# Differential attention with memory heads first and heads 4 to 7 projected by tokens, and a memory preparation in two parts

## The chip, the cores and the metric

The kernel runs on one core of one Trainium2 chip. The metric is the device time of one execution in microseconds (us), the median of several runs. The engines are named as in the profile: PE is TensorE (PEld its weight loads), DVE is VectorE, ACT is ScalarE, POOL is GpSimd and SP is SyncE, which here only issues transfers. A change of 0.2% is 2.8 us.

## The reference, cut to what matters

The program is a stack of transformer blocks on 256 tokens of width 1024, with feed-forward layers (d_ff 2816) and a different mixer in each block. The change touches the second mixer, differential attention with memory heads, and in one place the mixer after it, whose block prepares a second memory.

```
def diff_layer(h, w_in, lam_p, norm_g, w_out, mem_k, mem_v, slopes, layer_idx):
    proj = h @ w_in
    q = proj[..., :DIFF_QK].reshape(B, S, H, 2, Dh).transpose(0, 2, 3, 1, 4)
    k = proj[..., DIFF_QK:2 * DIFF_QK].reshape(B, S, H, 2, Dh).transpose(0, 2, 3, 1, 4)
    v = proj[..., 2 * DIFF_QK:2 * DIFF_QK + DIFF_V].reshape(B, S, H, 2 * Dh).transpose(0, 2, 1, 3)
    xq = proj[..., 2 * DIFF_QK + DIFF_V:]
    ...
    o = diff_attention(q, k, v, lam, slopes)     # per head: softmax(q0 k0) - lam * softmax(q1 k1), times v
    o = rmsnorm(o, norm_g, eps=SUBLN_EPS) * (1.0 - lam_init)
    o = o.transpose(0, 2, 1, 3).reshape(B, S, H * 2 * Dh)
    xo = memory_attention(xq, mem_k, mem_v)      # 4 heads of 128 against 256 memory rows
    return jnp.concatenate([o, xo], axis=-1) @ w_out
```

There are H = 8 heads, each with two components of Dh = 64, and h has 1024 features. All is float32.

## The kernel before

**Weights come in chunks.** Every weight matrix is cut into chunks of 128 x 2048 floats (1 MB), 234 in all. SP loads a chunk into one of three `raw` buffers; ACT rounds it to `w_hi` (L1493), and DVE writes the rest to `w_lo` (L1743), each in rings of three. PE multiplies three times for each tile: high by high, high by low, low by high.

**A chunk is used in one of two forms.** By columns (`columns_chunk`, L1134 to L1136) the weights are stationary and 256 tokens move, so that features come out on the partitions; one chunk holds 256 output columns and takes 48 products of 128x256 into one `prod` bank. DVE scales the bank by `rb` (the norm of each token, spread over the partitions by a small product and a copy, `spread`) and writes `q`, `k` or `xq`. By tokens (`tokens_chunk`, L1140 to L1144) the activations are stationary and 512 weight columns move, so that tokens come out on the partitions; two chunks (the halves of the 1024 features) give 512 output columns in two banks, one for each 128 tokens, with 24 products of 128x512 a chunk. ACT scales the banks by the token's norm (L1558) and writes `v`. The output projection (`down_chunk`) is by tokens too.

**Attention is cut into ticks.** `Plan.ticks` makes a pipeline over heads: a tick holds scores (S, L1338), the weights on DVE (F), the turning of the weights on PE (T, L1358) and its copy on ACT (L1678), the product with v (V, L1379 to L1397), and the low part of a finished memory tile on DVE (L, L1855). A differential head scores both components in one tick, in `acc` banks 0 and 1, each with 64 of the 128 rows of the array; the next tick has no scores. PE runs a tick in the middle of a chunk (`mid`) and one behind it (`end(slot)`). In the stage of the output projection (`pl.draining`), where the `acc` banks are taken, a tick scores one component at a time in `prod` bank 0. `HeadNorms` puts the norm of each head (ACT squares, POOL root, DVE scale) and, by pairs, the turning of the outputs (L1472) around the ticks.

**The order of the differential layer** is written out in `make_plan`: query and key of heads 0 and 1 by columns, the values of heads 0 to 3 by tokens (two chunks), query and key of heads 2 and 3, the values of heads 4 to 7, query and key of the last two pairs, two chunks of `xq`, and six chunks of output projection. Heads 0 to 7 come first in the ticks and the four memory heads last; these are scored between the chunks of the output projection. Before the layer stands `prep`, which turns x to features in four banks while DVE and ACT write `acts_h` (L1520) and `acts_l` (L1770).

**Moving by blocks.** In the feed-forward layers a middle tile is turned without PE: DVE transposes squares of 32 x 32 (L1904), and 16 transfers of 32 partitions, 8 issued by SP and 8 by POOL (`move_blocks`, L1004), put the squares on their partitions.

**In the mixer after it** `mem_prep` readies four tiles of the second memory ahead of the gate chunks (`rg`): ACT writes the high parts (L1668) and DVE the low parts (L1994); behind it DVE scales x (L2001), writes the `w_lo` of a chunk, and then the low part of an attention tile (L1855) for which PE's next V waits.

All engines take their work in the order of one list of items, and wait on semaphores.

Of the kernel before, what the change touches and what calls it, by code (L numbers as in the profile page):

```python
# [26 lines left out]
P = 128  # L27
D = 1024
# [93 lines left out]
class Plan:  # L122


    def __init__(self):
# [23 lines left out]
        self.early_half = False  # L149
        self.quartered = None  # L150
# [65 lines left out]
    def prep(self, gain, resid, last_down=None, double=False, wait=False):  # L216
        it = self.add("prep", gain=gain, resid=resid, first=self.acts, acts_free=self.acts_users,
                      x_new=self.x_new, y=self.y, y_chunk=self.y_chunk, x_turned=self.x_turned, n=self.stat,
                      double=double, wait=wait)
# [13 lines left out]
    def mem_prep(self, gain, kts, tiles, source):  # L233
        self.add("mem_prep", gain=gain, kts=kts, tiles=tiles, source=source, first=self.mem,
                 users=self.c if source == "mem2" else 0)
        self.mem += len(kts)

# [84 lines left out]
    def project_tokens(self, source, col, dest, at, of="x", mid=None, between=None):  # L322
        for k_half in range(2):
            self.chunk("rows_half", (*source, "half", (k_half, col)), mid, e=self.e, k_half=k_half, dest=dest, at=at,
                       of=of, acts=self.acts if of == "x" else self.mem, free=self.bank_free(2))
# [13 lines left out]


# [74 lines left out]
    def ready(self, units):  # L415
        for unit in units:
            unit["need"], unit["rope"] = self.read, self.rope_n
# [31 lines left out]
def unit_of(head, **k):  # L449
    return dict(dict(head=head, comps=1, tiles=1, v_width=P, out_tiles=1, out_row=0, tile=head, need=None,  # L450
                     need_v=None, is_out=False, closes=True, free=lambda: True, half=head % 2), **k)


def mem_units(heads, dims, q, layer=0):
    tiles = dims // P
    return [unit_of(h, shape=FULL, table=None, scale=1.0, q=(q, h * tiles),
# [5 lines left out]
class HeadNorms:  # L462
# [10 lines left out]
    def early(self):  # L473
        if self.scales >= 2 * (self.turns + 1) and not self.hold_turn:
            self.pl.head_turn(self.turns, self.which)
            self.turns += 1

    def late(self):
        if self.splits < self.turns:
            self.pl.head_lo(self.splits, self.which)  # L480
# [29 lines left out]
def make_plan():  # L510
# [77 lines left out]
    for _ in down:  # L588
# [10 lines left out]
    memory = mem_units(4, P, "xq", 1)  # L599
    heads = [unit_of(h, comps=2, shape=CAUSAL, table="alibi", scale=2.0 ** -(h + 1), q=("q", h), k=("k", h),  # L600
                     rows=None, v=("v", h * P), out="norm") for h in range(HEADS)]
    norms = HeadNorms(pl, heads, "diff")
    ticks = pl.ticks([[unit] for unit in heads + memory])
# [14 lines left out]
    query(0, None)  # L618
    pl.spread("x")
    key(0, None)  # L620
    pl.ready(heads[0:2])
    value(0)
    query(1)
    end(slot)
    key(1)
    end(slot)
    pl.ready(heads[2:4])
    value(2)
    for pair in (2, 3):
# [5 lines left out]
    for n in range(2):  # L635
        pl.project(w, 3 * D + n * COLS, "xq", 2 * n, mid=slot, factors=(P ** -0.5,) * 2)
        end(slot)
    pl.ready(memory)
    pl.ready_v(memory)
    pl.draining = True  # L640
    norms.hold_turn = True

    def memory_turned(n):
        if n == 2:
            norms.hold_turn = False

    downs(slot, "diff_w_out", 0, pairs_of(0, 1, 2, 4, 5, 3), memory_turned)
# [1598 lines left out]
```

## Time and profile before

| | us |
|---|---|
| median of 3 runs | 1418.22 (1418.0 to 1418.61) |
| the profiled execution, its time | 1418.27 |
| its span, first to last instruction | 1416.5 |
| PE busy | 1403.6 |
| differential layer on PE (683.65 to 826.61) | 142.96 |

The matmul durations of the profile overlap: a product of 128x512 lasts 0.39 us, but the next starts 0.23 us after it. What a chunk costs is therefore read from the starts of its products, not from their durations. The granted clock of PE is 0.999 of full speed over the span.

### The profile page before, as it was taken

What the parts mean: (1) busy time and instruction counts of PE and PEld (TensorE: products, weight loads), DVE (VectorE), ACT (ScalarE), POOL (GpSimd) and SP (SyncE); (2) the same over time, 40 slices, a digit from 0 to 9 for tenths busy, and PEclk for the clock granted to TensorE, in tenths of its full rate; (3) what the DMA queues carried; (4) which work ended last, traced back from release to release, by engine and by line L of the source; (5) the groups of instructions that cost most, each with busy time, mean ns of one, the idle gap of its engine ahead of it and who ended that gap; (6) DMA issues with size and microseconds to landing.
All of it is one profiled execution on the core that took longest, in us unless ns stands there. A gap on an engine that the chain in (4) does not pass through costs nothing.

```text
span 1416.5 us, 18653 instructions
## 1 busy us (share of the span) xinstructions
PE 1403.6 (99%) x7200; PEld 1190.3 (84%) x7200; DVE 857.3 (61%) x1035; ACT 704.9 (50%) x981; POOL 259.8 (18%) x504
## 2 busy tenths in 40 slices
PE   9999999999999999999999999999999999999998
PEld 7888889988888888888889888888887989888886
DVE  5656565756555565555656565555796655565554
ACT  6554454445444454444555555444555554644443
POOL 1022210002222222222012113222201100132222
PEclk9999999999999999999999999999999999999999
DMA  9765654455655656665544446665553553366562
GB/s 349 290 213 201 219 186 156 166 185 192 221 201 198 218 196 215 207 220 198 180 149 150 139 168 258 216 222 200 186 177 136 188 179 134 125 228 225 197 220 74
DMA packets 71655, 275.55 MB, mean 195 GB/s; under 512 B 17392, under 2 KB 37232, under 8 KB 40848
## 3 DMA queue, kind: packets, MB, share of 16 engines
q1 hardware_dynamic: 57168, 259.57, 51.6%
q0 software_dynamic: 14400, 14.81, 3.4%
q8 instruction: 57, 0.93, 0.3%
q14 instruction: 30, 0.25, 0.0%
HBM read 259.88 MB, written 1.05 MB: 184 GB/s over the span
## 4 chain that ended last, share of the span: by engine, by line
PE 95%; ACT 2%; DVE 1%; issue 1%; DMA 0%; POOL 0%; SPq 0%; DVEq 0%; POOLq 0%; ACTq 0%
PE prod L1140 16%; PE prod L1141 16%; PE prod L1144 15%; PE acc L1144 10%; PE acc L1140 10%; PE acc L1141 10%; PE prod L1134 5%; PE prod L1136 5%; PE prod L1135 5%; PE acc L1338 1%; PE acc L1159 1%; ACT w_hi L1493 1%; PE acc L1358 1%; DVE w_lo L1743 0%; PE o_bank L1394 0%
## 5 line engine op out<-in xcount | busy, mean ns | idle before, releaser
L1743 DVE TENSOR_TENSOR w_lo<-raw,w_hi 128x2048 fp32r<-128x2048 f32 x233 | 533.6, 2291 | 383.4 <-ACT w_hi L1493 380.8
L1493 ACT CAST w_hi<-raw 128x2048 fp32r<-128x2048 f32 x233 | 444.2, 1907 | 431.6 <-PE prod L1144 182.1
L1140 PE MATMUL prod<-w_hi,acts_h 128*128 128x512 f32 x944 | 370.2, 392 | 2.5 <-DVE w_lo L1752 1.8
L1144 PE MATMUL prod<-w_hi,acts_l 128*128 128x512 f32 x944 | 367.7, 389 | 0.0
L1141 PE MATMUL prod<-w_lo,acts_h 128*128 128x512 f32 x944 | 367.4, 389 | 0.0
L1004 POOL DMA_DIRECT2D four<-four x408 | 200.1, 498 | 602.4 <-DVE four L1904 585.3
L1140 PE MATMUL acc<-w_hi,mix_h 128*128 128x512 f32 x600 | 236.0, 393 | 0.0
L1144 PE MATMUL acc<-w_hi,mix_l 128*128 128x512 f32 x600 | 233.7, 390 | 0.0
L1141 PE MATMUL acc<-w_lo,mix_h 128*128 128x512 f32 x600 | 233.5, 389 | 0.0
L1140 PEld LDWEIGHTS prod<-w_hi,acts_h 128*128 128x128 f32 x944 | 177.2, 188 | 43.0 <-issue 6.9
L1144 PEld LDWEIGHTS prod<-w_hi,acts_l 128*128 128x128 f32 x944 | 177.2, 188 | 37.5 <-DVE acts_l L1814 0.3
L1141 PEld LDWEIGHTS prod<-w_lo,acts_h 128*128 128x128 f32 x944 | 177.3, 188 | 35.6
L1144 PEld LDWEIGHTS acc<-w_hi,mix_l 128*128 128x128 f32 x600 | 112.6, 188 | 23.7
L1140 PEld LDWEIGHTS acc<-w_hi,mix_h 128*128 128x128 f32 x600 | 112.7, 188 | 23.0
L1141 PEld LDWEIGHTS acc<-w_lo,mix_h 128*128 128x128 f32 x600 | 112.7, 188 | 22.6
L1134 PE MATMUL prod<-acts_h,w_hi 128*128 128x256 f32 x424 | 124.0, 293 | 1.1 <-ACT work L1558 0.7
L1136 PE MATMUL prod<-acts_h,w_lo 128*128 128x256 f32 x424 | 119.9, 283 | 0.0
L1135 PE MATMUL prod<-acts_l,w_hi 128*128 128x256 f32 x424 | 119.8, 283 | 0.0
L1573 ACT ACTIVATE four<-prod,stats 128x256 f32<-128x256 f32 x108 | 51.1, 474 | 115.4 <-PE prod L1144 103.3
L1134 PEld LDWEIGHTS prod<-acts_h,w_hi 128*128 128x128 f32 x424 | 81.1, 191 | 3.6 <-issue 2.4
L1074 POOL TENSOR_SCALAR stats<-stats 128x1 f32<-128x1 f32 x28 | 14.1, 505 | 373.9 <-ACT sq L1506 372.8
L1135 PEld LDWEIGHTS prod<-acts_l,w_hi 128*128 128x128 f32 x424 | 81.2, 191 | 0.4 <-issue 0.2
(277 smaller groups left out, 1261.7 us busy)
## 6 DMA issues: line engine op xcount, KB each, us to landing
raw<-in_weights_dram SPq DMA_DIRECT2D x234, 1024.0 KB, 5.0
four<-four SPq DMA_DIRECT2D x408, 16.0 KB, 2.1
four<-four POOLq DMA_DIRECT2D x408, 16.0 KB, 1.9
raw<-in_weights_dram SPq DMA_DIRECT2D x16, 256.0 KB, 6.9
work<-in_mem_dram POOLq DMA_DIRECT2D x2, 1024.0 KB, 13.5
grow<-in_gain_rows_dram POOLq DMA_DIRECT2D x4, 512.0 KB, 3.7
tabs<-in_tabs_dram POOLq DMA_DIRECT2D x1, 1632.0 KB, 9.9
work<-in_x_t_dram SPq DMA_DIRECT2D x4, 256.0 KB, 5.7
```

Of the source, the lines that this page charges most:

```text
L1004: engine.dma_start(mid_moved_to[32 * b:32 * b + 32, a * P:(a + 1) * P], mid_blocks[32 * a:32 * a + 32, b * P:(b + 1) * P]).then_inc(done, 16)
L1134: pe.matmul(out, wh, moving_hi, start=first, stop=False, skip_group_check=True)
L1135: pe.matmul(out, wh, moving_lo, start=False, stop=False, skip_group_check=True)
L1136: return pe.matmul(out, wl, moving_hi, start=False, stop=last, skip_group_check=True)
L1140: pe.matmul(out, still_hi, wh, start=first, stop=False, skip_group_check=True)
L1141: pe.matmul(out, still_hi, wl, start=False, stop=False, skip_group_check=True)
L1144: return pe.matmul(out, still_lo, wh, start=False, stop=last, skip_group_check=True)
L1159: mm = pe.transpose(bank[:, i * S + t * P:i * S + (t + 1) * P], x[:, t, kt * P:(kt + 1) * P], ident)
L1338: mm = pe.matmul(bank[:, at:at + width], dests[q][r0:r1, qt + n, t * P:(t + 1) * P], dests[k][r0:r1, kt + n, 0:width], start=(n == 0), sto ...
L1493: act.copy(w_hi[:, c % RING], raw[:, c % RAW]).then_inc(hi_done, 1)
L1573: act.activation(gate_s[:, t], up_bank(it, t)[:, 0:S], ACT.Silu, scale=rstd["x"][:, t:t + 1]).then_inc(silu_done, 1)
L1743: dve.tensor_tensor(w_lo[:, c % RING], raw[:, c % RAW], w_hi[:, c % RING].bitcast(F32), ALU.subtract).then_inc(lo_done, 1)
```

## The change

1. **Three projections go by tokens, and are turned to features afterwards.** `project_turned` replaces six chunks by columns (two of `xq`, two of q and two of k, for heads 4 to 7) with six by tokens. ACT writes the two banks, scaled, to a buffer `cut` (in `mem_k`) in groups of 32 columns; DVE transposes all squares of 128x1024 in one instruction into a second buffer (in `obuf`); 16 transfers of 32x256 (8 from SP, 8 from POOL) move them to `xq`, `q` or `k`. For keys (`keys=True`) the transpose writes runs of 32 neighbouring elements; for queries (`xq`, q) it writes every eighth element, and PE loads such a query tile with a step of eight floats (`tokens_of`), while keys are read in runs of 32 (`keys_of`).
2. **Factors.** Queries need a factor for each head: POOL makes products of the norm and the factor (`scales`, one for `xq`, four for q).
3. **Order.** `xq`, q and k of heads 4 to 7, their values, then q, k of heads 0 and 1, values of heads 0 to 3, q and k of heads 2 and 3, then the output projection in the order of pairs 4, 5, 2, 3, 0, 1. In the ticks the memory heads come first, then heads 4 to 7, then 0 to 3. `spread` moves behind the values.
4. **Memory preparation in two parts.** The low parts on DVE become an item of their own (`mem_low`), put behind the first gate chunk.
5. Waits on the transfers are added for the scores and for whatever overwrites what they read.

```diff
@@ class Plan
+    def project_turned(self, source, col, dest, at, buffers, keys, of="x", mid=None, between=None, scales=None):
+        for k_half in range(2):
+            self.chunk("rows_half", (*source, "half", (k_half, col)), mid, e=self.e, k_half=k_half, dest=dest, at=at,
+                       of=of, acts=self.acts if of == "x" else self.mem, free=self.bank_free(2), turned=self.turned,
+                       buffers=buffers, scales=scales, keys=keys)
...
+        self.turn_behind[self.c + RAW] = self.items[-1]
+        self.turned += 1
+        for t in range(2):
+            self.bank_reader.append(("cut_done", 2 * self.turned - 1 + t))
@@ make_plan, the differential layer
-    ticks = pl.ticks([[unit] for unit in heads + memory])
+    heads_in_order = heads[4:8] + heads[0:4]
+    ticks = pl.ticks([[unit] for unit in memory + heads_in_order])
...
+    pl.project_turned(w, 3 * D, "xq", 0, "diff", False, scales=pl.scales([P ** -0.5]))
+    pl.ready(memory)
+    pl.ready_v(memory)
+    pl.project_turned(w, 512, "q", 4, "diff", False,
+                      scales=pl.scales([2.0 ** (h + 1) * 64 ** -0.5 for h in range(4, 8)]))
+    end(slot)
+    pl.project_turned(w, D + 512, "k", 4, "diff", True, mid=slot, between=lambda: end(slot))
+    end(slot)
+    pl.project_tokens(w, 2 * D + 512, "v", 512, mid=slot, between=lambda: end(slot))
...
-    downs(slot, "diff_w_out", 0, pairs_of(0, 1, 2, 4, 5, 3), memory_turned)
+    downs(slot, "diff_w_out", 0, pairs_of(4, 5, 2, 3, 0, 1))
@@ make_plan, the gate chunks
-    pl.mem_prep("g_mem", [4, 5, 6, 7], [8, 9, 10, 11], "mem2")
+    prepared = pl.mem_prep("g_mem", [4, 5, 6, 7], [8, 9, 10, 11], "mem2", low=False)
     pl.add("scale_x", stat=pl.stat)
-    pl.project_tokens(w, 2560, "rg", 0, mid=slot, between=lambda: end(slot))
+
+    def gate_half():
+        end(slot)
+        pl.mem_low(prepared)
+
+    pl.project_tokens(w, 2560, "rg", 0, mid=slot, between=gate_half)
@@ build
+        def tokens_of(name, blocks, rows, tile, t):
+            if not blocks:
+                return dests[name][rows, tile, t * P:(t + 1) * P]
+            four_tiles = dests[name][:, tile // 4 * 4:tile // 4 * 4 + 4].rearrange("p a b -> p (a b)")
+            return four_tiles.rearrange("p (i t k) -> p k t i", t=2, k=4)[rows, tile % 4, t]
+
+        def move_features(engine, it, token_blocks, done):
+            to = dests[it["dest"]][:, it["at"]:it["at"] + 4].rearrange("p a b -> p (a b)")
+            engine.wait_ge(features_turned, it["turned"] + 1)
+            for a in token_blocks:
+                for b in range(4):
+                    engine.dma_start(to[32 * b:32 * b + 32, a * S:(a + 1) * S],
+                                     cut_buffer(it, 1)[32 * a:32 * a + 32, b * S:(b + 1) * S]
+                                     ).then_inc(done, 16)
@@ scores on PE
+                    if unit["moved"]:
+                        pe.wait_ge(early_features_moved, 128 * unit["moved"])
+                        pe.wait_ge(late_features_moved, 128 * unit["moved"])
@@ vector
+                        dve.wait_ge(cut_done, 2 * it["turned"] + 2)
...
+                        dve.transpose(blocks, cut).then_inc(features_turned, 1)
```

**DVE, the start of the differential layer, before.** From the last low activation tile on: `work` is q and k of heads 0 and 1, and L1867 is the mask and maximum of the first scores.

```order
L1770 SCALAR_TENSOR_TENSOR acts_l<-acc3,vecs,acts_h 128x256
L1743 TENSOR_TENSOR w_lo<-raw,w_hi 128x2048 [waits hi_done]
L1922 SCALAR_TENSOR_TENSOR work<-prod0,rb 128x256 [waits chunk_used,rb_done]
L1922 SCALAR_TENSOR_TENSOR work<-prod0,rb 128x256
L1743 TENSOR_TENSOR w_lo<-raw,w_hi 128x2048 [waits hi_done]
L1916 TENSOR_TENSOR work<-prod1,rb 128x512 [waits chunk_used,rb_done]
L1743 TENSOR_TENSOR w_lo<-raw,w_hi 128x2048 [waits hi_done]
L1867 ISA masked,small<-tabs,acc0 128x128 [waits score_done]
```

And after, from the same place: L2029 are the transposes of `xq` and of q, L1976 the maximum of the first memory head.

```order
L1883 SCALAR_TENSOR_TENSOR acts_l<-acc3,vecs,acts_h 128x256
L1856 TENSOR_TENSOR w_lo<-raw,w_hi 128x2048 [waits hi_done] x2
L2029 STREAM_TRANSPOSE obuf<-mem_k 128x4x8x32 [waits cut_done]
L1856 TENSOR_TENSOR w_lo<-raw,w_hi 128x2048 [waits hi_done] x2
L2029 STREAM_TRANSPOSE obuf<-mem_k 128x4x8x32 [waits late_features_moved,early_features_moved,cut_done]
L1976 TENSOR_REDUCE small<-acc0 128x2 [waits score_done]
L1856 TENSOR_TENSOR w_lo<-raw,w_hi 128x2048 [waits hi_done]
L1942 RECIPROCAL small<-small 128x2 [waits exp_done]
```

Two reads of `prod` banks for each pair of heads have become one transpose for each four tiles, and the first maximum stands directly behind a transpose that waits for ACT's cut.

**PE, the first chunk of the output projection, after.** `work` is q and k of head 2; `acc` is the projection; in the rows of before this stage scored only memory heads (`prod0<-mem_k,obuf`).

```order
L1225 MATMUL acc1<-w_hi,mix_l 128x512
L1422 MATMUL prod0<-work 128x128 [waits prod_read,max_done,late_features_moved,early_features_moved]
L1422 MATMUL prod0<-work 128x256
L1464 MATMUL prod1<-work,four 128x128 [waits prod_read,hn_scaled,turned_read,values_read]
L1465 MATMUL prod1<-work,four 128x128
L1466 MATMUL prod1<-work,four 128x128
L1221 MATMUL acc2<-w_hi,mix_h 128x512 [waits hn_scaled,turned_read]
```

The two components of heads 2 and 3 have moved into this stage, where each is scored alone, one at a stop: four stops with one component in place of two with both.

**DVE, the gate chunks, before.** L1994 is the low part of the memory, L2001 the scaling of x, L1855 the low part for which PE's V waits.

```order
L1855 TENSOR_TENSOR mix_l<-o_bank,mix_h 128x256 [waits o_hi]
L1994 SCALAR_TENSOR_TENSOR mix_l<-obuf,vecs,mix_h 128x256 [waits mem_hi] x4
L2001 TENSOR_SCALAR x_res<-x_res,stats 128x1024 [waits rstd_done,xf_done]
L2001 TENSOR_SCALAR x_res<-x_res,stats 128x1024
L1743 TENSOR_TENSOR w_lo<-raw,w_hi 128x2048 [waits hi_done,dve_step]
L1855 TENSOR_TENSOR mix_l<-acc3,mix_h 128x256 [waits o_hi]
```

And after:

```order
L1968 TENSOR_TENSOR mix_l<-o_bank,mix_h 128x256 [waits o_hi]
L2125 TENSOR_SCALAR x_res<-x_res,stats 128x1024 [waits rstd_done,xf_done]
L2125 TENSOR_SCALAR x_res<-x_res,stats 128x1024
L1856 TENSOR_TENSOR w_lo<-raw,w_hi 128x2048 [waits hi_done,dve_step]
L1968 TENSOR_TENSOR mix_l<-acc3,mix_h 128x256 [waits o_hi]
L1937 TENSOR_TENSOR four<-acc0,tabs 128x384 [waits turned,score_done]
L1937 TENSOR_TENSOR sq<-acc1,tabs 128x384 [waits o_done,score_done]
L2118 SCALAR_TENSOR_TENSOR mix_l<-obuf,vecs,mix_h 128x256 [waits mem_hi] x4
```

The four memory tiles have gone behind the low part that PE waits for.

## Rows read from the trace of the kernel before

**Rows 1.** The page, section 1: engine, busy us, share of span, instructions.

```profile
PE 1403.6 (99%) x7200; PEld 1190.3 (84%) x7200; DVE 857.3 (61%) x1035; ACT 704.9 (50%) x981; POOL 259.8 (18%) x504
```

**Rows 2.** Timeline of PE at four chunk starts: start, length, instruction.

```profile
860.61 0.39 PE L1140 MATMUL acc<-w_hi,mix_h 128*128 128x512 f32 x1
...
866.05 0.39 PE L1140 MATMUL prod<-w_hi,acts_h 128*128 128x512 f32 x1
...
1119.20 0.28 PE L1134 MATMUL prod<-mix_h,w_hi 128*128 128x256 f32 x1
...
1142.24 0.40 PE L1140 MATMUL prod<-w_hi,mix_h 128*128 128x512 f32 x1
```

**Rows 3.** What PE waited for: total us, times, longest.

```profile
PE acc L1379 <- DVE mix_l L1855: 0.9, 1, 0.9
PE prod L1134 <- ACT work L1558: 0.7, 1, 0.7
...
PE prod L1134 <- DVE acts_l L1770: 0.4, 2, 0.2
```

**Rows 4.** Timelines of PE and PEld at one head's scores and one memory head's.

```profile
699.93 0.93 PE L1338 MATMUL acc<-work 64*128 64x128 f32 x8
700.78 0.50 PE L1140 MATMUL prod<-w_hi,acts_h 128*128 128x512 f32 x1
...
700.25 0.38 PE L1338 MATMUL acc<-work 64*128 64x256 f32 x2
...
700.47 0.38 PE L1338 MATMUL acc<-work 64*128 64x256 f32 x2
...
700.14 0.20 PEld L1338 LDWEIGHTS acc<-work 64*128 64x128 f32 x2
...
700.26 0.20 PEld L1338 LDWEIGHTS acc<-work 64*128 64x128 f32 x2
...
785.44 1.02 PE L1338 MATMUL prod<-mem_k,obuf 128*128 128x256 f32 x4
786.30 0.27 PE L1358 MATMUL aux<-tabs,four 128*128 128x128 f32 x1
```

**Rows 5.** Groups by line and form: busy us, mean ns, idle before; then two DMA issues.

```profile
L1743 DVE TENSOR_TENSOR w_lo<-raw,w_hi 128x2048 fp32r<-128x2048 f32 x233 | 533.6, 2291 | 383.4 <-ACT w_hi L1493 380.8 <-POOL stats L1077 2.2
L1493 ACT CAST w_hi<-raw 128x2048 fp32r<-128x2048 f32 x233 | 444.2, 1907 | 431.6 <-PE prod L1144 182.1 <-PE acc L1144 166.8 <-PE prod L1136 76.2
L1004 POOL DMA_DIRECT2D four<-four x408 | 200.1, 498 | 602.4 <-DVE four L1904 585.3 <-issue 16.9
L1904 DVE STREAM_TRANSPOSE four<-four 128x512 f32<-128x512 f32 x51 | 36.3, 712 | 1.8
L1558 ACT ACTIVATE work<-prod,stats 128x512 f32<-128x512 f32 x8 | 5.2, 678 | 4.5 <-PE prod L1144 4.5
L1686 ACT ACT_TABLE_LOAD x4 | 5.1, 1283 | 0.1
L1863 DVE TENSOR_REDUCE small<-acc 128x2 f32<-128x512 f32 x7 | 4.8, 687 | 2.0 <-PE acc L1338 2.0
L1686 ACT ACTIVATE four<-acc,small 128x256 f32<-128x256 f32 x10 | 4.7, 474 | 3.9 <-DVE small L1863 3.7
L1678 ACT COPY four<-acc 128x512 f32<-128x512 f32 x6 | 3.5, 586 | 11.9 <-PE acc L1358 11.9
...
four<-four SPq DMA_DIRECT2D x408, 16.0 KB, 2.1
four<-four POOLq DMA_DIRECT2D x408, 16.0 KB, 1.9
```

**Rows 6.** Timelines of ACT, DVE and PE around the gate chunks, 1080 to 1089 us.

```profile
1080.34 1.90 ACT L1493 CAST w_hi<-raw 128x2048 fp32r<-128x2048 f32 x1
...
1082.95 1.68 DVE L1994 SCALAR_TENSOR_TENSOR mix_l<-obuf,vecs,mix_h 128x256 fp32r<-128x256 f32 x4 [5.64 <-ACT mix_h L1668]
...
1088.20 0.42 DVE L1855 TENSOR_TENSOR mix_l<-acc,mix_h 128x256 fp32r<-128x256 f32 x1
```

More of the change, by code:

```diff
@@ L231, in prep, with mem_prep, mem_low @@
             self.statistic("x", "x")
[L233 to L235 removed]
+    def mem_prep(self, gain, kts, tiles, source, low=True):
+        it = self.add("mem_prep", gain=gain, kts=kts, tiles=tiles, source=source, first=self.mem,
+                      users=self.c if source == "mem2" else 0)
         self.mem += len(kts)
+        if low:
+            self.mem_low(it)
+        return it
+    def mem_low(self, of):
+        self.add("mem_low", of=of)
     def post_norm(self, gain):
@@ L474, in early @@
         if self.scales >= 2 * (self.turns + 1) and not self.hold_turn:
-            self.pl.head_turn(self.turns, self.which)
+            self.pl.head_turn(self.units[2 * self.turns]["head"] // 2, self.which)
             self.turns += 1
@@ L598, in make_plan @@
     w = ("diff_w_in", 0)
-    memory = mem_units(4, P, "xq", 1)
+    memory = mem_units(4, P, "xq", 1, q_blocks=True)
     heads = [unit_of(h, comps=2, shape=CAUSAL, table="alibi", scale=2.0 ** -(h + 1), q=("q", h), k=("k", h),
-                     rows=None, v=("v", h * P), out="norm") for h in range(HEADS)]
-    norms = HeadNorms(pl, heads, "diff")
-    ticks = pl.ticks([[unit] for unit in heads + memory])
+                     rows=None, v=("v", h * P), out="norm", q_blocks=h >= 4, k_blocks=h >= 4) for h in range(HEADS)]
+    heads_in_order = heads[4:8] + heads[0:4]
+    norms = HeadNorms(pl, heads_in_order, "diff")
+    ticks = pl.ticks([[unit] for unit in memory + heads_in_order])
     slot = slots(ticks, norms)
@@ L616, in value @@
         pl.ready_v(heads[2 * pair:2 * pair + 4])
-    query(0, None)
-    pl.spread("x")
[L620 to L629, printed above, removed]
+    pl.project_turned(w, 3 * D, "xq", 0, "diff", False, scales=pl.scales([P ** -0.5]))
[7 more added lines that the diff above has]
+    pl.project_tokens(w, 2 * D + 512, "v", 512, mid=slot, between=lambda: end(slot))
+    pl.ready(heads[4:8])
+    pl.ready_v(heads[4:8])
+    end(slot)
+    pl.spread("x")
+    for pair in range(2):
         query(pair)
@@ L634, in make_plan @@
         pl.ready(heads[2 * pair:2 * pair + 2])
[L635 to L639, printed above, removed]
-    pl.draining = True
[L641 to L645, printed above, removed]
-    downs(slot, "diff_w_out", 0, pairs_of(0, 1, 2, 4, 5, 3), memory_turned)
+        if pair == 0:
+            value(0)
+    pl.draining = True
+    downs(slot, "diff_w_out", 0, pairs_of(4, 5, 2, 3, 0, 1))
     pl.draining = False
@@ L1100, in _ @@
                     move_blocks(pool, (2, 3), late_blocks_moved)
+                elif kind == "rows_half" and it["k_half"] and it.get("turned") is not None:
+                    move_features(pool, it, (2, 3), late_features_moved)
+                elif kind == "scales":
+                    pool.wait_ge(rstd_done, it["stat"])
+                    for n, factor in enumerate(it["factors"]):
+                        ins = pool.tensor_scalar(scales[:, 2 * (it["at"] + n):2 * (it["at"] + n) + 2], rstd["x"], factor,
+                                                 None, ALU.mult)
+                    ins.then_inc(scales_done, len(it["factors"]))
                 elif kind == "load_mem2":
```

97 lines of the change are left out of this document (85 added, 12 removed).

## The prediction, written before the changed kernel was run

> **What bounds the kernel now.** I read the shares of the engines first. PE is busy in 99% of the span [rows 1], so the time is PE's work in order plus its few waits, and any other engine costs only where PE waits for it. But a busy PE is not yet a price: its products overlap. So I read second, on the timeline, how far apart the starts of chunks lie. From 860.61 to 866.05 PE does one chunk by tokens, 24 products of 128x512, in 5.44 us. From 1119.20 to 1142.24 it does four chunks by columns, 192 products of 128x256, in 23.04 us: 5.76 us each [rows 2]. The durations in the groups would have said something else; the starts decide. Third, the list of PE's waits [rows 3]. Three of them lie where the change works: 0.4 us for the low activations and 0.7 us for ACT's write of v, both in the differential layer, and 0.9 us for a low attention tile in the gate chunks. They are single waits, so all that the change can give lies in the price of chunks and in these three.
>
> **Part 1, six chunks by tokens.** 6 x (5.44 - 5.76) = -1.9 us [rows 2]. All of it is on the path. This is small because the form by columns moves as many elements in all; only the cost of a start is saved.
>
> **Part 2, the wait for low activations.** By columns PE needs all eight activation tiles within one chunk; by tokens the first chunk needs four, and the second four are due 6.3 us after the layer's start, where I find them written after 5.7 us. The 0.4 us [rows 3] go: -0.4. The turning of the second half of x now stands 2.7 us into the chunk and finds its data there.
>
> **Part 3, the wait for v.** PE waited 0.7 us at a `prod` bank because ACT had exponentials of two heads, and earlier a table load of 1.28 us [rows 5], ahead of L1558. In the new order no tick stands in the last chunk of the first values, so ACT is free there; behind the second values the pattern is that of before, which had no wait. With a little of the switch, -0.8 us.
>
> **Part 4, the gate chunks.** DVE sat idle 5.64 us until ACT had written the memory's high parts, then did four low parts in 1.68 us, then the rest, and came to PE's tile at 1088.20 [rows 6]. The high weights were there since 1080.34 + 1.90 = 1082.24. Without the memory, DVE scales x in the idle time, starts `w_lo` at 1082.3, needs 2.29 us [rows 5] and is at PE's tile at about 1084.6, over 3 us before PE asks. The 0.9 us [rows 3] go. The four low parts come after the tick; the next `w_lo` is needed two chunks (10.9 us) later, so 1.7 us are covered, and nothing else reads them before the memory projection. If that cover were gone, they would cost 1.7 us. -0.9 us.
>
> **Part 5, scores of heads 2 and 3 between the chunks of the output projection.** The scores of a head with both components take 700.78 - 699.93 = 0.85 us [rows 4]. They run in pairs: two products start together at 700.25 and two at 700.47, one of each component, since each takes half of the array's rows. A component alone has no partner, but as many steps: it costs from 0.65 us (the steps 0.11, 0.11, 0.22, 0.22 of the pairs' starts) to 0.85. Four alone instead of two pairs: 4 x 0.65 - 1.7 = +0.9 to 4 x 0.85 - 1.7 = +1.7. I take the middle, +1.3, and +0.1 for one more interruption of the stream.
>
> **Part 6, new waits in the phase of the memory heads.** Times count from the layer's start on PE. This is where ACT and DVE get the most new work, and I walk it by rows 5. Projections of `xq` end at 11.8. ACT cuts (0.68 us a bank) by 12.6; the transpose has twice the elements of L1904, 0.71 us, so I estimate 1.25 us (0.53 us more for 512 more elements at the pace of 128 lanes that the row allows): 13.9. POOL issues 8 transfers of 0.5 us, to 18, and landing adds 1.9: 20. SP's eight wait behind a chunk and are as early. The first memory scores are due at 22.7, so this wait is hidden by q's two chunks with 2.7 us to spare. Behind POOL's transfers stand four factor products; they end at 20 to 22, when ACT wants to cut q at 20.0; that cut is due at 23.5. Queued behind SP's wait is the next chunk's load, which lands 1 to 4 us early even so.
>
> Then it becomes tight. ACT cuts q to 24.0, writes a `w_hi` of 1.9 to 25.9 and loads its table to 27.2; DVE waits for the cut, transposes to 25.3 and gives the first maximum (0.69) at 26.0; exponentials (two of 0.47 and their sums, 1.35) end at 28.6; the weights are ready at 29.5, PE turns them at 30.7. Each further memory head takes ACT 1.35 + 0.59 us and a small cast, and DVE its maximum, two multiplications and a low part, an estimate of 2 us, every 4 us of PE, beside 1.9 and 2.3 us for every chunk of 5.4. ACT reaches the cut of k only behind the fourth exponentials, at 39.2, and finishes its first bank at 39.9; PE wants that bank at 39.8, +0.2. The second V wants the first output's low part, which on DVE stands behind k's transpose: ready at 43.2, wanted at 42.7, +0.55. Together +0.75. After that PE does two chunks with hardly a tick and all catch up; the transfers of k land by 48, and head 4 is scored at 53. From below: both waits vanish if ACT is 0.6 us faster, 0. From above: each of the four ticks late by a `w_hi` share, as in the one wait of 0.7 us that ACT's queue makes now [rows 3], 4 x 0.7 = +2.8.
>
> **Part 7, queries read with a step of eight floats.** No row shows such a load. The nearest are the packed ones: a pair of loads starts 0.12 us after the one before [rows 4], and they feed products 0.22 us apart. From below 0, since they are hidden; if a load took twice as long, 0.24 us, it would still be hidden but for the two first products of a head and the first load of a memory head: about +0.25 for each of heads 4 to 7 and +0.1 for each memory head, +1.4. The packed row is the nearest, but nothing says that the step is free; I take +0.2.
> The Trainium skill (SBUF — State Buffer, Door 1: The DMA port swizzle) has a rule against this: SBUF has lines of 16 bytes, and every access that goes to a new line pays, so that float32 may step four elements at most for free. It gives no figure. By it part 7 is not near 0 but at the +1.4 of a doubling or above; it is the rival below.
>
> **The sum.** -1.9 - 0.4 - 0.8 - 0.9 + 1.3 + 0.1 + 0.75 + 0.2 = -1.65 us. The profiled execution took 1418.27 us (span 1416.5 and 1.8 around it) and is within 0.05 of the median 1418.22, so the forecast is 1416.6 us. A measurement of this kernel tells about 0.2%, 2.8 us, from no change: below 1415.4 is faster, above 1421.1 slower. The forecast is the same within that.
>
> **Rivals.**
> Faster: the new waits are nil and a component alone costs 0.65 us. -1.9 - 0.4 - 0.8 - 0.9 + 0.9 + 0.1 = -3.0, 1415.2 us; with the over-heads of switching between the two forms saved, 1414.5. For it: PE's queue shows only three waits in the whole stage before, and memory heads between projection chunks already run at one tick for each half chunk without one. Against: there ACT had no cut and no table load.
> Queues: ACT and DVE fall behind in the memory phase by the upper end, +2.8 instead of +0.75, and part 5 costs 1.7: 1416.6 + 2.05 + 0.4 = 1419.1 us. For it: the margins of part 6 are 0.1 to 2 us on a walk of 20 steps. A transpose that writes every eighth element slower than L1904 would do it, 1.25 us each time.
> Slower, the strided loads: one mechanism, at L1422 for the queries of heads 4 to 7 and of memory. The loads come to bind once one takes longer than the 0.22 us of its product, that is from a doubling of 0.12. At three times (0.33 to 0.36) a head costs 4 x 0.33 = 1.32 instead of 0.65, a memory head 1.32 instead of 0.86: 4 x 0.67 + 4 x 0.46 = +4.5, 1420.9 us; at four times +8, 1424.5. For it: nothing in the trace excludes it; against: the stage's loads are hidden twofold now.
> That the chunks do not get cheaper: then the transfers' and cuts' waits eat 1.9 us and it ends at 1418.5. The two prices come from long clean stretches, so this is unlikely, and I fold it into the queues.
>
> **How the numbers follow.** Forecast, 1415.5 to 1418: 0.47. Queues, 1418 to 1420.5: 0.20. Faster, 1413.5 to 1415.4: 0.21. Strided loads at three times or more: 0.12. Faster by over 0.2%: 0.21. Slower by over 0.2%: most of the strided case and a tail of the queues, 0.14. Within 0.2%: 0.65. The range for 8 in 10 runs from 1413.9 to 1420.8: it leaves out the far half of the strided case and the ends of the others.
>
> **What would show it.** Right: chunks of `xq`, q and k by tokens 5.44 us apart in starts; no PE wait for L1883 in the layer's first two chunks, none at the gate chunks; each of the four lone components of heads 2 and 3 at 0.65 to 0.85 us; waits of under 1 us in all between 20 and 50 us of the layer; scores of heads 4 to 7 at 0.85 to 1.1 us. Wrong: memory scores far over 0.86 us or heads 4 to 7 far over 0.85 (the step), PE waiting for DMA at the first memory scores (the transfers), for ACT's cuts at k's or the values' chunks or for a `mix_l` (the queues), or a wait in the last two projection chunks, where the norm of heads 2 and 3 now has less than a chunk and a half.

## The result and the profile after

The changed kernel takes 1423.54 us, the median of 5 runs (1423.2 to 1424.76), against 1418.19 us for the kernel before in the same session: a ratio of 1.0036, 95% interval 1.0025 to 1.0047. That is 5.3 us (0.4%) slower, outside the predicted range, whose upper end was 1420.8. The profiled execution took 1423.2 us, span 1421.4.

The page's section 1 of the changed kernel, and what its PE waited for (total us, times, longest):

```profile
PE 1407.9 (99%) x7056; PEld 1187.6 (84%) x7056; DVE 857.1 (60%) x1030; ACT 709.9 (50%) x993; POOL 265.3 (19%) x533
```

```profile
PE prod L1221 <- DVE four L2013: 3.8, 1, 3.8
...
PE prod L1215 <- DVE acts_l L1883: 0.2, 1, 0.2
```

The shares are within one point of those of [rows 1]. Of the three waits of [rows 3] the one for v and the one for the low tile at the gate chunks are gone. Of the one for low activations the half in the differential layer (0.2 us, at 687.93) is gone too; the other half stood in a later layer (at 1013.21) that the change leaves alone, and it is the 0.2 us that is left (at 1019.01). One wait is new and larger than all three together, and it does not lie in the layer that was changed: it is in the feed-forward layer behind it. The differential layer itself takes 143.8 us on PE (starts 683.55 to 827.37), against 143.0 before; the first stretch of the next layer takes 35.55 us (830.92 to 866.47) for chunks that take 30.48 before. So +0.9 us in the layer that was rewritten and +5.1 us behind it; less the 0.9 us that is gone at the gate chunks this comes to 5.1 us, and the spans of the two profiled executions differ by 4.9.

**Where the 3.8 us are made.** In that layer DVE transposes a block at 840.42, SP and POOL move it with eight transfers each, and ACT casts it. ACT's queue has this cast ahead of its read of the next projection (L1683); DVE's read of the same bank (L2013) follows, and only then is the bank free for PE's next projection. So PE does not wait for the moved tiles themselves, but for a bank whose readers stand behind them. The timelines of POOL, SP, ACT, DVE and PE of the changed kernel there:

```profile
843.96 4.03 POOL L1075 DMA_DIRECT2D four<-four  x8 [11.55 <-issue]
...
846.15 3.42 SPq L1106 DMA_DIRECT2D raw<-in_weights_dram  x2
...
852.11 0.71 ACT L1598 CAST mix_h<-four 128x256 fp32r<-128x256 f32 x2 [5.22 <-DMA four<-four]
852.73 0.83 ACT L1683 ACTIVATE four<-prod,stats 128x256 f32<-128x256 f32 x2
...
853.53 0.87 DVE L2013 SCALAR_TENSOR_TENSOR four<-prod,stats,four 128x256 f32<-128x256 f32 x2
...
854.15 0.77 PE L1221 MATMUL prod<-w_hi,acts_h 128*128 128x512 f32 x1 [3.83 <-DVE four L2013]
...
854.72 0.63 PE L1222 MATMUL prod<-w_lo,acts_h 128*128 128x512 f32 x1
```

and of POOL, SP and ACT of the kernel before, whose transpose ran at 839.62:

```profile
840.62 4.01 POOL L1004 DMA_DIRECT2D four<-four  x8 [8.99 <-DVE four L1904]
...
845.35 3.43 SPq L1035 DMA_DIRECT2D raw<-in_weights_dram  x2
...
846.56 0.71 ACT L1513 CAST mix_h<-four 128x256 fp32r<-128x256 f32 x2 [0.47 <-DMA four<-four]
```

Before, POOL starts 0.3 us behind the end of the transpose, released by it. After, it starts 2.8 us behind the end (841.13), and the view has only "issue" as what it waited for: the data were there and POOL did nothing. Its last three transfers (846.51 to 847.5) are issued behind SP's next weight load of 1 MB (846.15). They land only after that load has landed (851.5), 4.5 to 5.0 us after their issue; before, all of POOL's transfers were issued ahead of the load, and the longest of the move took 2.2. So 2.5 us on POOL become 4.7 at ACT's cast, counted from each kernel's transpose.

PE then pays twice. Its granted clock, by the view of windows (stretch, length, PE busy, clock, DMA share, GB/s):

```profile
852.00:854.00 2.00, 0.00 (x0) 0.90 0.69 291
854.00:856.00 2.00, 1.85 (x5) 0.50 0.04 8
856.00:858.00 2.00, 2.00 (x8) 0.75 0.20 44
858.00:860.00 2.00, 2.00 (x11) 1.00 0.24 59
```

After 3.8 us without work PE runs at 1.2 GHz, half of its clock, until 857: products start 0.43 us apart instead of 0.23 (854.72 to 855.14). That is the further 1.2 us of the 5.07.

**Why POOL was idle.** I counted the transfers that POOL issues, from 0, in both traces. In each, POOL stands still for about 3 us ahead of numbers 133 and 261. Before, number 261 is a load of the memory, that nobody waits for (timeline of POOL before, where the number before it is the last of the row above):

```profile
862.84 3.91 POOL L1004 DMA_DIRECT2D four<-four  x8 [7.34 <-DVE four L1904]
870.25 0.56 POOL L1103 DMA_DIRECT2D work<-in_mem_dram  x1 [3.49 <-issue]
```

The change lets POOL issue 24 transfers for xq, q and k. With them, number 261 is the first transfer of the first block move behind the layer. That is a correlation of two traces; the experiments put it to the test.

### The profile page after: what moved, and what is told of

It reads as the page before. It is cut to its first block, busy times and chain, and to the rows that moved or that the text cites. A ratio compares the mean times of both kernels' runs of the same rounds, so it can differ in the third digit from the quotient of the medians.

```text
span 1421.4 us, 18464 instructions
## 1 busy us (share of the span) xinstructions
PE 1407.9 (99%) x7056; PEld 1187.6 (84%) x7056; DVE 857.1 (60%) x1030; ACT 709.9 (50%) x993; POOL 265.3 (19%) x533
## 4 chain that ended last, share of the span: by engine, by line
PE 97%; DVE 1%; DMA 1%; issue 0%; ACT 0%; POOL 0%; SPq 0%; DVEq 0%; POOLq 0%; ACTq 0%
PE prod L1221 17%; PE prod L1225 17%; PE prod L1222 17%; PE acc L1221 10%; PE acc L1225 10%; PE acc L1222 10%; PE prod L1215 4%; PE prod L1217 4%; PE prod L1216 4%; PE acc L1422 2%; PE acc L1240 1%; PE acc L1443 1%; PE o_bank L1479 0%; PE o_bank L1482 0%; PE prod L1422 0%
## 5 line engine op out<-in xcount | busy, mean ns | idle before, releaser
L1221 PE MATMUL prod<-w_hi,acts_h 128*128 128x512 f32 x992 | 390.6, 394 | 4.8 <-DVE four L2013 3.8
L1225 PE MATMUL prod<-w_hi,acts_l 128*128 128x512 f32 x992 | 387.0, 390 | 0.0
L1222 PE MATMUL prod<-w_lo,acts_h 128*128 128x512 f32 x992 | 386.7, 390 | 0.0
L1221 PEld LDWEIGHTS prod<-w_hi,acts_h 128*128 128x128 f32 x992 | 186.7, 188 | 47.6 <-issue 9.8
L1222 PEld LDWEIGHTS prod<-w_lo,acts_h 128*128 128x128 f32 x992 | 186.7, 188 | 37.5
L1683 ACT ACTIVATE four<-prod,stats 128x256 f32<-128x256 f32 x108 | 51.0, 475 | 117.3 <-PE prod L1225 105.4
L1215 PE MATMUL prod<-acts_h,w_hi 128*128 128x256 f32 x328 | 96.0, 293 | 0.2 <-DVE acts_l L1883 0.2
L1217 PE MATMUL prod<-acts_h,w_lo 128*128 128x256 f32 x328 | 92.7, 283 | 0.0
L1216 PE MATMUL prod<-acts_l,w_hi 128*128 128x256 f32 x328 | 92.7, 283 | 0.0
L2013 DVE SCALAR_TENSOR_TENSOR four<-prod,stats,four 128x256 f32<-128x256 f32 x108 | 51.7, 481 | 34.6 <-ACT four L1683 32.6
L1215 PEld LDWEIGHTS prod<-acts_h,w_hi 128*128 128x128 f32 x328 | 62.8, 191 | 1.4 <-issue 0.7
```

Of the source, the lines that this page charges most:

```text
L1215: pe.matmul(out, wh, moving_hi, start=first, stop=False, skip_group_check=True)
L1216: pe.matmul(out, wh, moving_lo, start=False, stop=False, skip_group_check=True)
L1217: return pe.matmul(out, wl, moving_hi, start=False, stop=last, skip_group_check=True)
L1221: pe.matmul(out, still_hi, wh, start=first, stop=False, skip_group_check=True)
L1222: pe.matmul(out, still_hi, wl, start=False, stop=False, skip_group_check=True)
L1225: return pe.matmul(out, still_lo, wh, start=False, stop=last, skip_group_check=True)
```

## Experiments on the new wait

**24 transfers in the kernel before, and 24 memsets as a control.** Everything else is as before.

```diff
     pl.prep("norm_g11", 0.5, pl.last_down)
+    pl.add("pad", n=24)
...
+                elif kind == "pad":
+                    for n in range(it["n"]):
+                        pool.dma_start(spare[0:32, 4 * n:4 * n + 4], tabs[0:32, 16:20]).then_inc(padded_done, 16)
```

The control has `pool.memset(spare[:, n:n + 1], 0.0)` there.

> The kernel before, with 24 small transfers (32 rows of 16 bytes, into a spare buffer that nobody reads) issued by POOL ahead of the differential layer, and nothing else of the change. In both traces POOL issues nothing for about 3 us ahead of its transfers number 133 and 261 (counted from 0). In the changed kernel number 261 is the first transfer of the first block move of the feed-forward layer behind the differential layer, and PE waits 3.83 us for that move; in the kernel before number 261 falls elsewhere. Theory A (every 128th transfer that POOL issues is held up for some 3 us, and the 24 feature transfers that POOL issues for q, k and xq moved this point onto the move): these 24 transfers do the same to the kernel before, its first move there is 3 us late, PE waits 3 to 5 us on its products, and the time is 1421.2 to 1423.3 us. Theory B (the wait comes from the new order of the differential layer, its clock, its weight loads or its reads): 1418.2 us, within 0.5.

> The kernel before, with 24 POOL memsets of one column each in the place where the run with 24 transfers has its transfers. Theory A (the hold-up goes by POOL's transfers): their number is that of the kernel before, POOL's hold-up stays where it was, 1418.2 us within 0.5. Theory C (it goes by the length of POOL's instruction stream, which is fetched in pieces, so that any 24 more instructions move it): POOL's hold-up moves too, and the time is 1419 to 1423 us.

Measured: 1425.14 us with the transfers (ratio 1.0045, 1.0032 to 1.0058), 1418.88 with the memsets (1.0001, 0.9993 to 1.0010). PE's waits and POOL's timeline with the transfers:

```profile
PE prod L1147 <- DVE four L1907: 4.0, 1, 4.0
...
843.74 4.01 POOL L1007 DMA_DIRECT2D four<-four  x8 [11.52 <-issue]
```

and what POOL waited for with the memsets:

```profile
POOL work L1108 <- issue: 3.0, 1, 3.0
```

Nothing of the changed layer is in this kernel, and it shows the same wait at the same move. With the memsets the hold-up stays at the load of the memory. So it goes by transfers, not by the length of POOL's stream: theory A stands, B and C fall. The time came out above theory A's upper end by 1.8 us. The half clock behind the wait gives most of it, by the windows of this kernel:

```profile
854.00:856.00 2.00, 1.93 (x5) 0.50 0.03 8
856.00:858.00 2.00, 2.00 (x6) 0.50 0.24 56
858.00:860.00 2.00, 2.00 (x7) 0.67 0.25 59
```

The half clock lasts until past 859 here (products start 0.43 us apart up to 859.33, in the changed kernel up to 856.85), and from 856 to 860 PE starts 10 products where it starts 15 in the changed kernel: 5 x 0.23 = 1.2 us. (The counts of the windows are higher, since a product that runs across the edge counts in both.) The wait is only 0.1 us longer. Nor is it a matter of the kernel alone: two of its five executions took 1423.93 us, the other three 1425.14 to 1425.57. What such a stall costs is thus not fixed by its length, and what decides it stays open.

**One transfer more in the changed kernel.** The same edit with n=1 (and rows of 64 bytes).

> The changed kernel, with one small transfer more (32 rows of 64 bytes, into a spare buffer) issued by POOL ahead of the differential layer. Theory A (by the number of the transfer): the first transfer of the feed-forward layer's first move is number 262 now, number 261 is the last feature transfer of k, some 5 us ahead of its reader, so PE's wait of 3.83 us on L1221 goes and the time is 1418.0 to 1419.5 us. Theory B (the new order of the layer) and theory C (the length of the stream, changed by one instruction): 1423.5 us, within 0.5.

Measured: 1418.26 us (0.9998, 0.9989 to 1.0006), 5.3 less than the changed kernel. POOL's timeline at the end of k's feature move and at the block move:

```profile
725.33 3.45 POOL L1041 DMA_DIRECT2D work<-obuf  x7 [10.71 <-DVE obuf L2036]
731.20 0.50 POOL L1041 DMA_DIRECT2D work<-obuf  x1 [2.42 <-issue]
...
841.31 4.02 POOL L1078 DMA_DIRECT2D four<-four  x8 [8.98 <-DVE four L2024]
```

The hold-up has gone to the eighth transfer of k, which is number 261 now, and nobody waits there: it lands at 734.27, and the first scores that read it start at 737.42. A kernel with one useless instruction more is 5.3 us faster; PE's stretch from 830.81 on takes 30.47 us, as before the change. This is the clearest proof that the whole step of 5.1 us belongs to that one number.

**What is counted: transfers or rows.** 24 transfers of one row (`spare[0:1, ...]`) instead of 32.

> The run with 24 small POOL transfers in the kernel before, each of them of 1 row instead of 32. Theory A1 (the hold-up comes at every 128th transfer, whatever its size): as with 32 rows, the first transfer of the move behind the differential layer is number 261, PE waits 3 to 5 us for the move, 1423 to 1425 us. Theory A2 (it comes at every 4096th row, that is descriptor, of POOL's transfers, and 128 moves of 32 rows make up that number): 24 rows shift it by less than one transfer, the hold-up stays where the kernel before has it, 1418.5 us within 0.6.

Measured: 1423.91 us (1.0039, 1.0025 to 1.0053). POOL's timeline:

```profile
843.46 4.03 POOL L1007 DMA_DIRECT2D four<-four  x8 [11.52 <-issue]
```

24 rows or 768, the same transfer is late: theory A1. It is the number of transfers.

**What it costs at other places.** 8 and 16 transfers instead of 24.

> The kernel before with 8 small POOL transfers (32 rows) ahead of the differential layer. POOL's transfer number 261 is then the first of the third block move of the feed-forward layer behind it (each move has eight of POOL). In the trace of before the cast that reads the third move starts 11.7 us after its transpose and waits for nothing. Theory A (one transfer at a fixed count is held up by 3 us, and it costs what the slack there leaves): the hold-up is seen at the third move, nobody waits, 1418.6 us within 0.6. Rival (the transfers ahead of the layer disturb its memory or weight traffic, whatever their count): slower in proportion, 1420 us or more.

> The same with 16 small POOL transfers: number 261 is the first of the second block move, whose reader, the cast on ACT, waits 1.09 us for it as it is. Theory A: the cast is about 3 us later than before and PE, that has less queued than a move takes, waits: 1420 to 1423 us. Rival (only the first move of a layer has no slack): 1418.6 us within 0.6.

Measured: 1418.65 us with 8 and 1418.64 us with 16 (both 0.9999, 0.9990 to 1.0008). POOL's timelines, with 8 and with 16, and ACT's with 16:

```profile
866.13 1.96 POOL L1007 DMA_DIRECT2D four<-four  x4 [10.09 <-issue]
```

```profile
855.14 1.96 POOL L1007 DMA_DIRECT2D four<-four  x4 [9.87 <-issue]
...
863.41 0.71 ACT L1520 CAST mix_h<-four 128x256 fp32r<-128x256 f32 x2 [5.44 <-DMA four<-four]
```

The hold-up stands at the third and at the second move, where the count puts it. At the second I was wrong: ACT's cast waits 5.44 us, 4.3 more than before, but PE does not wait. It has a chunk of the feed-forward layer's down projection to do there, which reads the tile of the first move (24 products, from 861.25 to 866.69), and DVE has read the bank that PE needs next by 865.7. At the first move the order holds no such chunk yet, only projections that need the bank. So of the three places only the first move of the layer has no slack on PE. "Its reader waits" is not "PE waits".

**All feature transfers on SP.** This takes POOL's 24 transfers away.

```diff
                 if c in plan.turn_behind:
                     move_features(sp, plan.turn_behind[c], (0, 1), early_features_moved)
+                    move_features(sp, plan.turn_behind[c], (2, 3), late_features_moved)
...
-                elif kind == "rows_half" and it["k_half"] and it.get("turned") is not None:
-                    move_features(pool, it, (2, 3), late_features_moved)
```

> The changed kernel with all 16 transfers of each feature move issued by SP, none by POOL. Theory A: POOL's count is that of the kernel before again, its hold-up goes to a place with slack, PE's wait of 3.83 us goes: 1418.0 to 1418.8 us, if SP's eight further issues (some 40 ns to 0.1 us each) do not make its weight loads late; if they do, there are waits for w_lo or w_hi around 690 to 730 us and the time is 1419 to 1420 us. Theory B (POOL's count has nothing to do with it): 1423.5 us.

Measured: 1424.71 us (1.0042, 1.0030 to 1.0055). By the time alone theory B would have won. The profile says otherwise: what PE and POOL waited for, and the timelines of SP and PE.

```profile
PE acc L1421 <- issue: 4.0, 2, 3.6
...
POOL work L1183 <- issue: 2.9, 1, 2.9
```

```profile
705.64 3.12 SPq L1038 DMA_DIRECT2D obuf<-obuf  x5
...
712.19 10.01 SPq L1038 DMA_DIRECT2D work<-obuf  x16
...
710.21 2.07 PE L1421 MATMUL acc<-mem_k,obuf 128*128 128x256 f32 x4 [3.55 <-issue]
```

The wait behind the layer is gone and POOL's hold-up is back at the load of the memory, as theory A says. But SP needs 10.01 / 16 = 0.63 us for one issue, where I had written 40 ns to 0.1 us without a row. The issues of the sixteen of xq end at 708.76, the last of them lands at 710.0, and the first memory scores wait 3.55 us for it; then PE's granted clock is 0.50 again, from 710.2 to 713.6. One stall was traded for another of about the same size. POOL's share of these issues, 0.5 us each, is what keeps xq in time.

## Experiments on the strided queries

Both start from the changed kernel with one transfer more, so that the stop is out of the way.

**Packed loads.** The weight loads read 128 neighbouring floats, which are not the queries of the tile: this kernel leaves out the right order of the queries, and only prices the load.

```diff
-            return four_tiles.rearrange("p (i t k) -> p k t i", t=2, k=4)[rows, tile % 4, t]
+            return four_tiles.rearrange("p (k t i) -> p k t i", t=2, k=4)[rows, tile % 4, t]
```

> The changed kernel with the one transfer ahead of the layer (1418.3 us), in which the weight loads of the queries xq and q of heads 4 to 7 read 128 neighbouring floats instead of one in eight; they are the wrong queries, the rest is unchanged. The trace of the changed kernel has 1.26 us for the scores of each of heads 4 to 7 against 0.85 us for heads 0 and 1. Theory S (the stride of 32 bytes in the stationary operand makes the load longer than the product that covers it): the four heads take 0.85 us each, 1.6 to 2.0 us less, 1416.3 to 1416.7 us. Rival (the 0.41 us is a matter of the moving keys in runs of 32 or of the waits there): no change, 1418.3 us within 0.4.

Measured: 1416.29 us (0.9983, 0.9974 to 0.9992), 2.0 less than with the stride, or 2.1 if each is taken against the kernel before in its own session (1418.49 and 1418.66 us).

**The queries laid packed by their transfers.** First q of heads 4 to 7, then xq too (`it["dest"] in ("q", "xq")`).

```diff
-    pl.project_turned(w, 512, "q", 4, "diff", False,
+    pl.project_turned(w, 512, "q", 4, "diff", True,
...
+            runs = to.rearrange("p (n a i) -> p a n i", n=8, a=4)
...
+                    if it["dest"] == "q":
+                        engine.dma_start(runs[32 * b:32 * b + 32, a],
+                                         cut_buffer(it, 1)[32 * a:32 * a + 32, b * S:(b + 1) * S]
+                                         .rearrange("p (n i) -> p n i", n=8)).then_inc(done, 16)
+                        continue
...
-            return four_tiles.rearrange("p (i t k) -> p k t i", t=2, k=4)[rows, tile % 4, t]
+            if name == "q":
+                return four_tiles.rearrange("p (t k i) -> p k t i", t=2, k=4)[rows, tile % 4, t]
```

> The changed kernel with the one transfer ahead of the layer, q of heads 4 to 7 turned like k (the transpose writes neighbouring floats) and laid by its 16 transfers in runs of 32 tokens, so that the 128 queries of a tile and head are neighbours when they are loaded. Nothing is left out. Theory S: the scores of heads 4 to 7 take 0.85 us, and the transpose of q 1.25 us instead of 2.2: 1416.4 to 1416.9 us. Rival (a transfer of 32 rows is 256 pieces of 128 bytes now, and they are slow): the heads' first scores wait, or POOL's issue of the eight transfers takes longer, 1418.3 us or more; where POOL's hold-up falls tells whether it goes by transfers (last of k's, as with one transfer more) or by pieces (earlier).

> The changed kernel with the one transfer ahead of the layer and both xq and q of heads 4 to 7 turned like k and laid by their transfers in runs of 32 tokens. Nothing is left out. Theory S (each load of a strided stationary operand costs): the run with runs of q alone gave 1416.7 us and the one with packed loads of both (wrong queries) 1416.3 us; this gives 1416.2 to 1416.6 us. Rival (xq's reader has no slack, since the memory scores start right behind its move, and transfers in 256 pieces of 128 bytes land later): PE waits for xq ahead of the first memory scores, 1417 to 1419 us.

Measured: 1416.72 us for q alone (0.9987, 0.9978 to 0.9996) and 1416.34 us for both (0.9985, 0.9976 to 0.9995). The views of the line of the scores and of the transposes (count: ns min/median/max), of the changed kernel and then of the one with both; the first and second row of each are the heads' queries and xq:

```profile
L1422 PEld LDWEIGHTS acc<-work x48: 182/320/334, 737.5 to 777.7; 64*128 64x128 f32 x48
...
L1422 PEld LDWEIGHTS acc<-mem_k,obuf x16: 316/328/338, 706.0 to 718.4; 128*128 128x128 f32 x16
...
L2029 DVE STREAM_TRANSPOSE obuf<-mem_k x3: 1247/2195/2198, 696.3 to 723.8; 128x1024 f32<-128x1024 f32 x3
```

```profile
L1437 PEld LDWEIGHTS acc<-work x48: 182/187/188, 737.1 to 775.6; 64*128 64x128 f32 x48
...
L1437 PEld LDWEIGHTS acc<-mem_k,obuf x16: 187/188/189, 706.0 to 718.0; 128*128 128x128 f32 x16
...
L2044 DVE STREAM_TRANSPOSE obuf<-mem_k x3: 1246/1246/1246, 696.3 to 723.5; 128x1024 f32<-128x1024 f32 x3
```

A load of 128 columns takes 0.32 us with a step of eight floats and 0.19 us packed. What that costs is read from starts, of a head of the changed kernel and of the same head with both packed:

```profile
745.12 1.33 PE L1422 MATMUL acc<-work 64*128 64x128 f32 x8
746.38 0.55 PE L1443 MATMUL acc<-tabs,four 128*128 128x128 f32 x3
```

```profile
744.31 0.93 PE L1437 MATMUL acc<-work 64*128 64x128 f32 x8
745.17 0.55 PE L1458 MATMUL acc<-tabs,four 128*128 128x128 f32 x3
```

1.26 against 0.86 us. Four heads make 1.6 us; the four memory heads' scores take 3.63 us in all with the step and 3.12 packed, 0.5. Together 2.1 us, against 1.9 to 2.1 between the measured times: theory S. The transfers in 256 pieces of 128 bytes did not hold anybody up: their median to landing is 1.9 us on POOL's queue, 1.7 to 1.8 in the changed kernel. In the kernel with runs of q the hold-up still stands ahead of number 261, although eight of the transfers before it are in 256 pieces: once more transfers are counted. It has little room there. Behind SP's weight load number 261 lands at 737.74 in that kernel, and at 736.71 in the one with both, each time 0.35 us ahead of the first scores of head 4. A little later, and this stop too would have reached PE.

The kernel with both leaves nothing out and is 7.2 us under the changed one and 2.4 us (0.15%) under the one before. That is less than the 0.2% that the prediction set as its resolution, but the interval excludes 1.

## The gate chunks alone

The fourth part of the change by itself, on the kernel before.

```diff
-    pl.mem_prep("g_mem", [4, 5, 6, 7], [8, 9, 10, 11], "mem2")
+    prepared = pl.mem_prep("g_mem", [4, 5, 6, 7], [8, 9, 10, 11], "mem2", low=False)
...
-    pl.project_tokens(w, 2560, "rg", 0, mid=slot, between=lambda: end(slot))
+
+    def gate_half():
+        end(slot)
+        pl.mem_low(prepared)
+
+    pl.project_tokens(w, 2560, "rg", 0, mid=slot, between=gate_half)
```

> The kernel before with one part of the change alone: the low halves of the second memory preparation are subtracted between the two gate chunks of the cross-attention layer instead of ahead of both. The trace of the changed kernel has no wait of PE for the gate there any more (0.92 us before). Theory D (part 4 of the prediction was right): 1417.2 us, 0.8 to 1.1 less than the kernel before. Rival: the gap closes but the gate's next reader or the next chunk waits instead, 1417.9 to 1418.4 us.

Measured: 1417.73 us (0.9995, 0.9986 to 1.0004). The time does not tell the two expectations apart. DVE's timeline does:

```profile
1085.21 0.42 DVE L1866 TENSOR_TENSOR mix_l<-acc,mix_h 128x256 fp32r<-128x256 f32 x1
...
1086.47 1.67 DVE L2006 SCALAR_TENSOR_TENSOR mix_l<-obuf,vecs,mix_h 128x256 fp32r<-128x256 f32 x4
```

The tile that PE waited for is written at 1085.2 instead of 1088.2 [rows 6], the four low parts follow behind it, and PE has no wait at the gate. The mechanism is shown; how much of the 0.9 us reaches the end is only bounded.

## Why the prediction was wrong, step by step

**The step that failed is one that is not in the sum.** Part 6 followed POOL's 24 new transfers through the layer, up to where k's land, and stopped there. It treated a transfer as 0.5 us of POOL and 1.9 us to landing, with nothing left behind. What they left behind was a shift of the count: POOL's stop of 3 us moved onto the first block move of the next layer, the only one of the three tried that has no slack on PE. It cost 5.07 us: 3.83 of waiting and 1.2 at half the clock. No rival had this mechanism either, so the upper end of the range was too low. The trace of before showed both stops and the wait of 0.47 us that ACT has at that move; nobody waited for them there, so I did not ask what sets their place.

**Part 7 was mis-sized.** +0.2 taken, 2.1 us by the starts and 1.9 to 2.1 by the runs. It lies between the two cases of the prediction, a doubling at +1.4 and three times at +4.5. I chose by the nearest row, the packed loads, while the text itself said that nothing in the trace makes the step free. The rule of the Trainium skill (SBUF — State Buffer, Door 1: The DMA port swizzle), that float32 may step four elements at most for free, spoke for +1.4 or more and was right in direction; the runs give the price for eight.

**Part 1** held: 84 products with nothing between them from 687.08 to 706.24, 5.47 us for 24, where 5.44 was taken. **Parts 3 and 4** held: the waits for v and at the gate are gone. **Part 2** held in kind, but its size was read wrong: I put both waits of that row in the differential layer, and only one of them, 0.2 us, was there. So it gave 0.2, not 0.4. **Part 5** came out at its upper end. The timeline of a lone component of heads 2 and 3 in the changed kernel, and what follows it:

```profile
788.62 0.92 PE L1422 MATMUL prod<-work 64*128 64x128 f32 x4
789.47 0.49 PE L1464 MATMUL prod<-work,four 128*128 128x128 f32 x2
```

0.85 us, as long as the pair of both takes; four times that against 1.7 is +1.7, not +1.3. **Part 6** was 0, not +0.75: between 706 and 737 us no PE wait stands in the view; every chunk there runs within 0.33 us of its products' pace. The transpose into steps of eight took 2.2 us instead of the 1.25 I had worked out (the one of k, into neighbours, took 1.25), and even that was covered.

With these sizes the sum is -1.9 - 0.2 - 0.8 - 0.9 + 1.7 + 0.1 + 2.1 = +0.1 us for the kernel without the stop on the move; the run with one transfer more is 0.2 us under the kernel before. With the stop it is +5.2, and +5.3 was measured. Without the step of eight floats it is -2.0, and -2.4 was measured. The terms thus close within 0.4 us. The median of the kernel before itself moved from 1418.19 to 1418.70 us between the sessions, so this is as close as these medians repeat.

## What to carry to other kernels

A DMA that is added on POOL also renumbers every later one: look in the trace for stretches in which POOL idles on "issue" ahead of a transfer, count their numbers, and see which transfer gets this number now and whether PE has work queued behind it. Ask of such a stall where PE, not the next reader, runs dry, and add the time at half the clock behind it (1.2 us behind 3.83 us here, some 1.2 us more than that in another kernel). Price a load of the stationary operand with a step of eight floats at 1.7 times the packed one and see whether the product still covers it, or let the transfer that lays the data pack them.

## What the hardware showed unexpectedly

- POOL stops for about 3 us ahead of its transfers number 133 and 261, in all thirteen traces (before, changed, and the eleven experiments), whether the added ones have 1 or 32 rows or 256 pieces. The distance is 128, but number 389 follows the one before it by 0.5 us in ten of the traces and by 1.0 us in the other three, so it is not every 128th, as the expectations had it. The Trainium skill (DMA: Bandwidth & Descriptors, SWDGE vs HWDGE vs iDMA) says that for POOL's transfers descriptors are written into rings in SBUF. That such a ring wraps or is refilled there would fit a count of transfers, but no run shows it, and it would have to say why two stops and no third, and why neither 1 row in place of 32 nor 256 pieces moves them. It stays open.
- A stop of 2.5 us on POOL became 4.7 us at ACT's cast, since one weight load of 1 MB got ahead of POOL's last three pieces (landing 5.0 us at most, 2.2 before).
- A PE stall of 3.83 us was followed by products at a granted clock of 0.50 for about 3 us: 1.2 us on top. Behind a stall of 3.96 us in another kernel it was about 5 us.
- SP takes 0.63 us to issue a small SBUF-to-SBUF transfer, POOL 0.5.
- DVE's 128x1024 transpose takes 2.20 us writing every eighth float and 1.25 us writing neighbours; a load of 128 columns for PE takes 0.32 and 0.19 us.
